# A transformer block on one core: the opening in groups of 4, 4, 4, 2 and 2 tiles, with the last gate pair in it, and the last attention head beside the projection

## The reference

```
mod = silu(c) @ w_ada + b_ada            # six vectors of 2048
h   = rms_norm(x, norm1_w) * (1 + scale1) + shift1
proj = h @ w_in                          # columns: q_a k_a v_a | q_f k_f v_f f_logit | g_a g_f
y_a = swa_sink_attention(rope(norm(q_a)), rope(norm(k_a)), v_a, sinks) @ w_o_swa    # 8 heads, 2 kv
y_f = forgetting_attention(norm(q_f), norm(k_f), v_f, log_sigmoid(f_logit + b)) @ w_o_fox   # 8 heads
merged = sigmoid(g_a) * y_a + sigmoid(g_f) * y_f
x = x + gate1 * (merged @ w_out)
h2 = rms_norm(x, norm2_w) * (1 + scale2) + shift2
g, u = split(h2 @ w_ffn_in)
out = x + gate2 * ((silu(g) * u) @ w_ffn_out)
```

## Time and profile before

| what | value |
|---|---|
| median of 3 runs | 2676.13 us (2676.12 to 2676.44) |
| the profiled execution | 2676.34 us |
| its span, first to last instruction | 2674.7 us |
| mean granted clock of PE | 0.989 |
| PE, DVE, ACT, POOL busy | 98%, 75%, 39%, 12% of the span |
| matmuls | 17066 |
| HBM read, written | 414.80 MB, 69.73 MB |

### The profile page before, as it was taken

How to read it: one execution, slowest core, us unless ns; L and a number is a source line. 1 busy time by engine, 2 the same in 40 slices (tenths; PEclk the granted TensorE clock), 3 DMA queues, 4 the chain that set the end, 5 groups by cost and what they waited for, 6 DMA issues and landing times.

```text
span 2674.7 us, 44661 instructions
## 1 busy us (share of the span) xinstructions
PE 2627.8 (98%) x17066; PEld 2394.5 (90%) x17066; DVE 1996.8 (75%) x3101; ACT 1042.5 (39%) x1420; POOL 311.0 (12%) x290
## 2 busy tenths in 40 slices
PE   6999999999999999999999999999999999999998
PEld 5778888888888888888899999999999999999998
DVE  7888888843333367755568888888888888888896
ACT  4333333433333322222354444444444444433443
POOL 0033223210010011123100000000000000010100
PEclk8899999999999999999999999999999999999999
DMA  9957676433333277777434544544544569495763
GB/s 335 319 174 205 189 204 193 145 109 95 103 96 101 78 231 236 235 233 234 148 94 157 161 137 157 164 136 154 166 138 151 166 206 341 166 348 181 261 219 119
DMA packets 399677, 487.18 MB, mean 182 GB/s; under 512 B 19220, under 2 KB 338984, under 8 KB 398984
## 3 DMA queue, kind: packets, MB, share of 16 engines
q1 hardware_dynamic: 361520, 352.47, 42.2%
q0 software_dynamic: 32896, 127.28, 13.5%
q10 hardware_dynamic: 5080, 4.85, 0.5%
HBM read 414.80 MB, written 69.73 MB: 181 GB/s over the span
## 4 chain that ended last, share of the span: by engine, by line
PE 91%; DVE 3%; DMA 2%; issue 2%; ACT 1%; SPq 1%; DVEq 0%; ACTq 0%
PE bank L924 15%; PE bank L927 15%; PE bank L926 15%; PE bank L601 12%; PE bank L603 12%; PE bank L602 12%; DMA ramp_w<-in_w_ada 2%; PE bank L753 1%; DVE ramp_acc L1386 1%; PE bank L779 1%; SPq L502 1%; DVE ada_acc L1338 1%; PE bank L742 1%; PE bank L873 1%; PE bank L875 1%
## 5 line engine op out<-in xcount | busy, mean ns | idle before, releaser
L924 PE MATMUL bank<-mov,w_slot 128*128 128x256 f32 x3472 | 980.3, 282 | 1.1 <-ACT blocks L1229 1.1
L927 PE MATMUL bank<-mov,w_slot 128*128 128x256 f32 x3472 | 978.8, 282 | 0.0
L926 PE MATMUL bank<-mov,w_slot 128*128 128x256 f32 x3472 | 978.6, 282 | 0.0
L924 PEld LDWEIGHTS bank<-mov,w_slot 128*128 128x128 f32 x3472 | 661.6, 191 | 1.4 <-ACT blocks L1229 1.3
L926 PEld LDWEIGHTS bank<-mov,w_slot 128*128 128x128 f32 x3472 | 662.1, 191 | 0.0
L927 PEld LDWEIGHTS bank<-mov,w_slot 128*128 128x128 f32 x3472 | 661.6, 191 | 0.0
L601 PE MATMUL bank<-h_hi,w_hi 128*128 128x512 f32 x1280 | 506.2, 395 | 0.0
L603 PE MATMUL bank<-h_hi,w_lo 128*128 128x512 f32 x1280 | 500.0, 391 | 0.0
L602 PE MATMUL bank<-h_lo,w_hi 128*128 128x512 f32 x1280 | 499.0, 390 | 0.0
L1317 DVE TENSOR_TENSOR w_lo<-w_raw,w_hi 128x1024 fp32r<-128x1024 f32 x192 | 245.2, 1278 | 325.7 <-ACT w_hi L954 325.1
L1168 ACT ACTIVATE w_slot<-w_raw 128x768 fp32r<-128x768 f32 x248 | 209.6, 845 | 542.9 <-PE bank L927 538.3
(11 more groups left out here) (250 smaller groups left out, 2839.1 us busy)
## 6 DMA issues: line engine op xcount, KB each, us to landing
w_raw<-in_w_ffn_in SPq DMA_DIRECT2D x352, 256.0 KB, 3.1
w_raw<-in_w_ada SPq DMA_DIRECT2D x128, 512.0 KB
w_raw<-in_w_ffn_out SPq DMA_DIRECT2D x88, 512.0 KB, 5.8
u_fm<-u_stage POOLq DMA_DIRECT2D x22, 1792.0 KB, 8.4
mov<-u_fm POOLq DMA_DIRECT2D x22, 1792.0 KB, 22.1
ramp_w<-in_w_ada SPq DMA_DIRECT2D x64, 512.0 KB, 8.8
w_raw<-in_w_in SPq DMA_DIRECT2D x128, 256.0 KB
w_raw<-in_w_in SPq DMA_DIRECT2D x64, 512.0 KB
```

The costliest lines, as they stand in the source:

```text
L924: nc.tensor.matmul(dst, lhsT=wh, rhs=xh, start=s == 0 and t == 0, stop=False, skip_group_check=True)
L926: nc.tensor.matmul(dst, lhsT=wh, rhs=xl, start=False, stop=False, skip_group_check=True)
L927: mm = nc.tensor.matmul(dst, lhsT=wl, rhs=xh, start=False, stop=last, skip_group_check=True)
```

## The change

**The opening.** The 16 tiles of h come in groups of 4, 4, 4, 2 and 2 (`RG`). A chunk of w_ada (four k rows of tiles) is now 512 columns wide in the first three groups, 2 KB of a row, and 256 in the last two; three slots hold chunks, and chunk n waits for the MACs of chunk n - 3. MACs are 1024 elements wide in the first three groups (48 of them) and 512 in the last two (32). PE makes all 16 normalised tiles at once, over seven banks, and ACT copies them to `xn` in SBUF; h is made from there. The first units have six column tiles in place of four: the two of the last gate pair of g_f run along in banks 2 and 3, 21 matmuls a tile, and the slices of w_in are 768 columns wide. Their sigmoids are taken by ACT at the end of the opening and written to `gate_fm` by ACT's own queue. The order on DVE stands in two tables, `h_behind` and `w_behind`: tile k's low part, or slice p's, stands behind MAC m of group p'. The column sums of group g stand behind the first unit of tile k by `COLS_BEHIND`. Two constant rows for the forget logic are loaded from `consts` and copied by ACT instead of set by DVE.

**The end of B and the start of C.** Head pair 7 has 4 units in place of 8. The window probabilities of head 7 are turned behind C's first unit and multiplied by the values behind its second. C takes the FoX heads first and the window heads second in every iteration.

```diff
+RG = (4, 4, 4, 2, 2)
+RG0 = (0, 4, 8, 12, 14)
+R_SLOTS = 3
+GW = 6 * P
...
+B_LAST = 4
...
+        NORM_BANKS = (0, 1, 2, 3, 5, 6, 7)
+        COLS_BEHIND = {2: 1, 6: 2, 9: 3, 12: 4}
...
+            def load_chunk(c):
+                p, j = divmod(c, STEP)
+                w = RG[p] * P
+                for b, c0 in enumerate((D, 0)):
+                    sp.dma_start(chunk(c)[:, b], w_ada_k[:, j * UK:(j + 1) * UK, c0 + RG0[p] * P:c0 + RG0[p] * P + w]
+                                 ).then_inc(chunk_landed[c % R_SLOTS], 16)
...
+            first_behind = {2: 0, 5: 1, 6: 2, 8: 3, 9: 4, 12: 5, 13: 6, 16: 7}
+            for n in range(STEP * len(RG)):
+                if n >= R_SLOTS:
+                    sp.wait_ge(ada_mac, macs_to(n - R_SLOTS))
+                load_chunk(n)
+                if n in first_behind:
+                    p = first_behind[n]
+                    if p == 1:
+                        sp.wait_ge(xn_ready, KD)
+                    if p >= 2:
+                        split(p - 2)
+                    load_first(p)
...
-            normalised(0)
-            for p in range(G_N):
-                ramp_cols(p)
-                if p:
-                    first_unit(p - 1, 1)
-                else:
-                    pe.wait_ge(fl_ready, 1)
-                first_unit(p, 0)
-                if p < G_N - 1:
-                    normalised(p + 1)
-            first_unit(G_N - 1, 1)
+            for k in range(KD):
+                normalised(k)
+            ramp_cols(0)
+            pe.wait_ge(xn_copied, KD)
+            pe.wait_ge(fl_ready, 1)
+            for k in range(KD):
+                first_unit(k)
+                if k in COLS_BEHIND:
+                    ramp_cols(COLS_BEHIND[k])
...
+                    if i == 0 and j != 2:
+                        pe.wait_ge(o_ready, (2 * HQ, 2 * HQ + 1, None, 2 * HQ + 2)[j])
+                    hi, lo = ((of_hi, of_lo), (oa_hi, oa_lo))[j // 2]
                     gemm(C_R + C_N * i + j, C_R + j, hi, lo, UK * (j % 2),
                          ((2, 3), (0, 1))[j // 2], j % 2 == 0, j % 2 == 1)
-                    if j == 2:
+                    if i == 0 and j == 0:
+                        probabilities(swa_pt, 2 * HQ)
+                    if i == 0 and j == 1:
+                        weighted_values(swa_blocks, 2 * HQ)
+                    if j == (3 if i == 0 else 2):
                         cols_of_step(ADA_C + i)
...
+            def first_high(p):
+                act.wait_ge(g_landed[p % 2], 32 * (p // 2 + 1))
+                if p >= 2:
+                    act.wait_ge(unit_done, p - 1)
+                nc.scalar.activation(first_hi(p)[:], g_raw[p % 2][:], ACT.Copy).then_inc(hi_done, 1)
...
+            w_behind = {(1, 1): 0, (1, 7): 1, (1, 12): 2, (2, 6): 3, (2, 12): 4, (3, 10): 5, (3, 14): 6, (4, 14): 7}
...
             split(ph_a, 0, 0 - LEAD, False)
+            act.wait_ge(gate_done, 1)
+            for t in range(2):
+                nc.scalar.activation(tile(rot, A_I + t), bank[2 + t][:], ACT.Sigmoid).then_inc(gate_out, 1)
             act.wait_ge(weights_ready, 1)
             act.wait_ge(y0_done, 1)
             y_evict(0, 6, first_evicted)
...
+                if last:
+                    low_output(tile(of_lo, h), tile(of_hi, h), 2 * h + 1)
+                    masked(swa_blocks, swa_at, swamask, 2 * h + 2, 8 * h + 8, h)
+                    normalise(swa_blocks, 2 * h + 2, h)
+                    return
```

More of the change, by code:

```diff
@@ L346, in ahead @@
             j += LEAD
-            if j < ph["n"]:
+            n = B_LAST if last and ph is ph_b else ph["n"]
+            if j < n:
                 return ph, i, j
             if not last:
-                return ph, i + 1, j - ph["n"]
+                return ph, i + 1, j - n
             if ph is ph_d:
                 return None
-            return after[id(ph)], 0, j - ph["n"]
+            return after[id(ph)], 0, j - n
         def numbers(ph, i, j):
@@ L759, in _ @@
                 late = 1 if h == 0 else 0
-                for j in range(B_N):
+                for j in range(B_N if h < B_I - 1 else B_LAST):
                     if j == 0:
@@ L804, in _ @@
             for i in range(C_I):
-                pe.wait_ge(o_ready, 2 * HQ + 2)
                 for j in range(C_N):
@@ L1114, in exponentials, with gate @@
                 ex.then_inc(p_done, 1)
-            def gate(b, n):
+            last_gates = xn[:, (KD - 2) * S:KD * S]
+            def gate(b, n, dst=gst):
                 for t in range(2):
-                    g = nc.scalar.activation(tile(gst, t), bank[b + t][:], ACT.Sigmoid)
+                    g = nc.scalar.activation(tile(dst, t), bank[b + t][:], ACT.Sigmoid)
                 g.then_inc(act_evicted, 1)
@@ L1124, in high_output, with swa_turned @@
                 nc.scalar.activation(dst, bank[4][:], ACT.Copy).then_inc(o_hi_done, 1)
+            def swa_turned(h):
+                act.wait_ge(p_turned, 2 * h + 2)
+                nc.scalar.activation(pt[:, 4 * P:7 * P], bank[6][:, 0:3 * P], ACT.Copy).then_inc(pt_act, 1)
             def head_pair(h, last):
-                for j in range(B_N):
+                for j in range(B_LAST if last else B_N):
                     split(ph_b, h, j, last)
@@ L1140, in head_pair @@
                     if j == 6:
-                        act.wait_ge(p_turned, 2 * h + 2)
-                        nc.scalar.activation(pt[:, 4 * P:7 * P], bank[6][:, 0:3 * P], ACT.Copy).then_inc(pt_act, 1)
+                        swa_turned(h)
+                if last:
+                    act.wait_ge(unit_done, B_R + B_N * h + B_LAST)
+                    gate(2, 0, last_gates)
+                    high_output(tile(of_hi, h), 2 * h + 1)
+                    exponentials(swa_blocks, 2 * h + 2, h)
+                    return
                 high_output(tile(oa_hi, h), 2 * h + 2)
@@ L1151, in merge @@
                     split(ph_c, i, j, last)
+                    if isinstance(i, int) and i == 0 and j == 0:
+                        swa_turned(HQ - 1)
+                    if isinstance(i, int) and i == 0 and j == 1:
+                        high_output(tile(oa_hi, HQ - 1), 2 * HQ)
                     if j == 3:
```

305 lines of the change are left out of this document (174 added, 131 removed).

## The result

The changed kernel takes **2680.05 us** in the median (2677.12 to 2681.58), the kernel before 2676.14 us (2675.13 to 2677.51) in the same comparison: a ratio of 1.0013, 95% interval 1.0007 to 1.0018. That is slower, though within what I had called "same"; the forecast was 2670.1 us and the range ended at 2677.

A forecast was written before the change was run, and what follows sets the result against it. Outside the opening PE's own work was taken to bound; in the new opening, PE from the first k step on, no longer DMA. -21.8 + 15.5 + 1.0 - 0.9 = -6.2 from 2676.3 gave 2670.1 us, range 2663 to 2677.

The forecast's parts named there:

- Parts 1, 3, 4: Last gate pair leaving head 7, -21.8 us; seam to phase A, +1.0; last head beside the projection, -0.9.
- Part 2, transfers: Opening: w_ada in 2 KB pieces moves at 390 GB/s, bounds 352 and 404; 2.1 MB come on top.
- pieces of 2 KB bring no rate: First rival, opening: transfers stay at 352 GB/s, +6.2 us, 2676.3 us, no change; chance 0.14.
- Part 2, first k step: Opening: after group 0's MACs and column sums, the first new k step starts at 54.1 us.
- Part 2, waits: Opening: PE idles 2.0, 2.0 and 3.9 us at the column sums of groups 1 to 3, together 7.9 us.
- Part 2, clock: Opening: half clock costs 2.3 us at the first step and 8.3 us around the column sums of groups 1 to 4.
- upper value: Opening: clock loss of 3.4 us per column-sum place with idle ahead, 1.75 in the sums, 1.65 in the next step.
- The bounds: Opening's +15.5 us: +9 without clock loss beyond the first step, +22 with upper clock values and 352 GB/s.
- the clock stays down: Rival, opening: half clock for 10 us after each of four column sums, +13 us, 2683 us; chance 0.07.

The follow-up runs named there:

- experiment 6: The changed kernel with the 2 KB pieces of groups 0 to 2 cut into two transfers of 1 KB pieces each: 2681.9 us.
- Experiment 12: Changed kernel with unread matmuls filling PE's waits, except ahead of the last two clusters, and low parts of slices 6 and 7 moved later: 2666.05 us.
- experiments 1 and 2: Changed kernel with unread matmuls filling PE's waits around the column sums, 2670.2 us; the same without the 18 behind the first column sums, 2672.85 us.
- Experiment 5: Changed kernel with the grouping undone: eight groups of two tiles, 1 KB pieces, gate pair still in the opening: 2670.75 us.
- 11: Changed kernel with eight pairs, early first step, filler matmuls ahead of clusters, second w_in slice loaded early into its own buffer: 2665.1 us.
- experiment 8: Changed kernel with eight pairs, second group's MACs not waiting for normalised tiles, first column sums between tiles 7 and 8: 2668.8 us.
- experiment 3: Changed kernel with column-sum clusters 2 to 5 cut to one pair of matmuls, waits and other work kept, outputs wrong: 2664.15 us in one run.

## Why the prediction was wrong

**Parts 1, 3, 4: right.** -21.9 us measured behind the opening, -21.7 forecast. The four units are gone, the wait in phase A's first iteration grew by 1.0 us (5.5 to 6.5; I had said 1.0), the wait at L742 is gone. These three were not tried one by one.

**Part 2, transfers: right, and worth less than it seems.** 384 GB/s against the 390 that I took, 352 from 18 to 24 us. The rival "pieces of 2 KB bring no rate" falls by experiment 6, and its price falls too: 2.4 us at the opening's end, not 6.2, since the later MACs had slack. The Trainium skill (HBM Reference, Specifications (TRN2)) says that a core streaming alone measures well above its share of about 358 GB/s; the 384 GB/s of this one core agree with that, and not with the rule that I had weighed in the prediction's first rival.

**Part 2, first k step: 58.2 instead of 54.1.** Group 0's MACs ended at 46.6, not 44.9: VectorE waited for its last two chunks, and the MACs on the last began at 41.7, not 40.1. Its column sums took 6.4 us, not 3.5 (+2.9). The chain behind them was 0.5 shorter than I had it.

**Part 2, waits: right.** I had derived 2.0, 2.0 and 3.9 us ahead of groups 1 to 3 from the order of the program; the trace has 2.25, 2.77 and 4.09, +1.2 together. Experiment 12 shows that the last is what I took it to be. One price in the working is off without effect: by the slope as stated the low part of 1536 elements takes 1.75 us, not 1.69 (1.76 in the trace).

**Part 2, clock: the step that failed.** From 58.2 us to the end, 113.1 us were used where I had 105.6. The column sums of groups 1 to 4 took 6.84 + 6.71 + 3.12 + 1.70 = 18.4 us, and I had put 10.5: **+7.9**. With the first group's +2.9 that is 10.8 of the 11.6 us by which the opening missed. The k steps, with waits taken off, used 85.6 us against my 76.6 + 2.3 + 8.3 = 87.2, so the clock loss that I had charged was about right for the steps and left none for the clusters. The working has a plain error in it besides: for the upper value I let a cluster of 3.5 us at half clock cost 1.75 more; at half clock it takes twice as long, +3.5 (measured +3.3). And for the first cluster I had assumed full clock, although the kernel before showed its own first cluster at half (in the filled version of that kernel it shrank from 3.57 to 1.95 us), with a wait ahead of it as now. The cause is shown by experiments 1 and 2: with the waits ahead of the clusters filled, those of groups 1 to 4 take their full-clock time and the opening is 9.5 and 11.8 us shorter.

The bounds were also added up too narrowly. By the terms of the working itself, no clock loss beyond the first step gives 15.5 - 8.3 = +7.2, not +9, and the upper clock values (+3.5) with 352 GB/s (+6.2) give +25.2, not +22. The +27.0 measured lie outside both.

**The rival that came true** is "the clock stays down". It said 10 us of half clock after each of the four column sums of groups 1 to 4; counted with the clusters there were 10.2, 10.2, 6.8 and none, and 17.1 around group 0's, which it had left out. It put the opening's end past 166 us; it was 171.3. Its 2683 us were somewhat high: the fourth cluster, with no wait ahead, lost nothing, and the 4 us of waits that it took to be hidden were not. I gave it 0.07 because "the steps between are dense". They are, but they come behind the wait and the cluster, and PE was already at half clock when they began.

What was not asked at all is whether grouping by four pays. Experiment 5 says that as it stands it does not: eight pairs are 9.3 us faster. Grouping by four delays the first k step, and doubles the cluster that follows each wait. With the waits filled and two low parts moved (12), groups of four come within 1 us of the best pairs (11), so much of that loss is the clock and the order, not the grouping as such. In experiment 5 and in experiment 8 something else of the change shows too: sixteen normalised tiles ahead of the first column sums are off the path only as long as group 0's MACs end behind them (they end at 42.95, the MACs at 46.6 us, in the changed kernel); with pairs they were in the way, by up to 5.4 us of the first step.

The Trainium skill (TensorE: Matmul & The Clock Gate, Why this matters for your kernels) advises against idle gaps of PE between bursts of matmuls. The trace agrees that gaps matter, since filling them kept the clock at 0.91 or more; what experiment 3 adds is that the work right behind a gap of 2.2 us decides as well.

What stays open: why a wait of 3.62 us without a long cluster dropped the clock for 6.8 us in experiment 3, and one of 4.09 us in the same run (ahead of 122.42) for 3.4 us (granted clock 0.64 from 122 to 126 us, 0.93 from 126 to 130). One run does not tell. Parts 1, 3 and 4 are confirmed only by their sum and by the two waits named.

## What to carry to other kernels

A wait of 2 to 4 us is priced by what stands behind it as well as by its own length: column sums behind such a wait ran at half clock here and were followed by more of it, so count them at twice their time, or fill the wait where PE is what bounds. Where the transfers bound, the fillers gained nothing. A rate gained on the transfers is worth only what they bound: here 2.4 us, while the larger groups put off the first use by 8.8 us. Where an engine stands waiting for something that another engine makes only behind a later step (VectorE for the high part of a slice, here), look at what stands behind that wait in its order and move the waiting instruction past it (experiment 12).

## What was new about the hardware

- Sixteen fp32 matmuls of 128x128 on one column took 3.6 us at the upper clock and 6.8 at the lower. Behind a wait of 2.25 us they were at the lower level from their first matmul on, and the chip stayed there for 10 us, through 3.4 us of dense 128x512 matmuls too. Behind fillers a cluster of sixteen ran at full clock and the dip of some 3 us came behind it; a cluster of eight without a wait ahead (the changed kernel's last, at 155 us) had no dip at all.
- 80 fillers of 0.23 us each in the waits kept PE's granted clock at 0.91 or more in every stretch of some 20 us from 47 us on. In the opening of the kernel before, 46 of them gained nothing.
- Pieces of 1 KB moved 351 GB/s, of 2 KB 385, on the same queue and into the same buffers (experiment 6 and the changed kernel, 24 to 46 us).
